# Moving the last projection of an attention stage into the next unit's first steps, and splitting the mixes by halves of the tokens

## The chip, the cores and the metric

One core of one Trainium2 chip. The metric is the device time of one execution in microseconds. The kernel before takes 2609.04 us, the median of 3 runs (2607.76 to 2612.22).

## The reference

A decoder trunk of two layers on 1024 tokens of 1024 features, in float32. Each layer computes

```python
hn = rms_norm(h, g)
proj = hn @ w_in     # q, k, v of 4 dilated heads and 4 pairs of differential heads, and cb, cc, ch
o_a = dilated_mixture_attention(aq, ak, av)           # 256 columns
o_b = rms_norm(differential_attention(...)) * scale   # 512 columns
o_c = cb * causal_dwconv(cc * ch, conv_w)             # 256 columns
h = h + concat([o_a, o_b, o_c]) @ w_out
h = h + conv_glu_ffn(rms_norm(h, g2), w_up, conv_w, w_down)
```

and a last rms_norm ends it. The change touches the attention stage, between `h @ w_in` and `@ w_out`, once per layer.

## The kernel before, in words

Everything lies with features on the 128 partitions and tokens along the free dimension; `h` is 8 tiles of 128x1024. A product in float32 is made of three passes: each operand x is rounded to a head (`x_hi`, `w_hi`) and a rest (`x_lo`, `w_lo`), and a half of a projection (`project_half`, L751: one tile of 128 output columns, one half of the tokens) is 8 x 3 = 24 matmuls of 128x512 (L747 to L749).

The mix has 8 tiles ("units"): 0 and 1 are pairs of dilated heads, 2 to 5 pairs of differential heads, 6 (`C0`) and 7 (`C1`) the gated convolution. Units 0 to 5 attend, one after the other; each takes 8 steps, one for 128 queries. `FINAL` is 5, the last attending unit. The order of work is written out by hand, one program for each engine, and the engines meet at semaphores. In a step i of unit u TensorE (`attention`, L1008) issues the scores of step i + 1 (L962, L963), turns the first group of probabilities (`turn_group`, L975), does one half of a projection for a later unit, and then attends (`attend_group`, L988). In step 0 it also turns v (L994), and in step 0 or 1 the heads of the unit before (L1004). ScalarE (L1258) copies turned probabilities out of PSUM (L1192), takes the exponentials of step i + 1 (L1233), and copies q, k, v and heads (L1200 to L1227, L1246). VectorE (L1573) masks scores and finds their top (`tops`, L1505), forms the probabilities (`shares`, L1513 to L1522), evacuates a projection's half (L1388), and between these norms the last unit's heads (`norm_heads`, L1421 to L1529), rotates q and k, makes the rests of the next unit's q and k (L1485 to L1492, after which `cur_ready` lets TensorE begin that unit's scores), and runs the convolution and its gate (`gate_out`, L1550).

`DURING` names the projections done beside unit 0 to 4, four each, two steps for each. The last is `(C1, GATED_B)`, the gate of the second convolution tile, in steps 6 and 7 of unit 4. Unit 5 has none. In its steps 2 to 7 TensorE computes the output projection of three column tiles ("early", `EARLY`) from the 7 tiles of the mix that are ready, 21 matmuls for each half (L1042). Before that the mixes must be split in head and rest in `x_hi` and `x_lo`, which the projections read until the last of them is done. GpSimd (L696 to L698, L676) splits mixes 0, 1, 2; ScalarE takes the heads (L1256) and VectorE the rests (L1554) of 3 and 6 in step 0 and 4 and 7 in step 1, all over the whole 1024 tokens, after `half_done` says that all projections are done. GpSimd otherwise splits the weight tiles in program order (`split`, L539 and L541; two slots): the first output tile before the mixes, the second right behind them. The sync queue reloads `h` behind the mix splits (`load_h`, L462) and issues the weight tiles from the third output tile on behind that.

## Time and profile before

| | us |
|---|---|
| median of 3 runs | 2609.04 |
| the profiled execution, time | 2612.52 |
| the profiled execution, span | 2610.7 |
| TensorE busy (share of the span) | 2437.4 (93%) |
| VectorE busy | 1522.6 (58%) |
| ScalarE busy | 880.9 (34%) |
| GpSimd busy | 1192.4 (46%) |
| mean granted TensorE clock | 0.967 |

Of the chain that ended last, TensorE has 69%, VectorE 20%, ScalarE 4%. Busy shares are averages over stages; what counts for a change in one stage is which wait ends last there. A wait stands in a row as "[idle before <-releaser]": the engine stood idle that long before this instruction, and what it waited for last. Names in rows are PE for TensorE, DVE for VectorE, ACT for ScalarE, POOL for GpSimd.

### The profile page before, as it was taken

The numbers are of one execution on the slowest core, as the hardware profiler recorded it, in microseconds if no ns is written. First come the engines' busy times: TensorE is split into PE (matmuls) and PEld (weight loads), VectorE is DVE, ScalarE is ACT, GpSimd is POOL, SyncE is SP. The second block draws the span as 40 slices with busy tenths as digits, with TensorE's granted clock in tenths as the row PEclk, the third lists the DMA queues.
The fourth block names the chain that finished last, engine by engine and source line by source line (L and its number), as shares of the span: only waits on it lengthen the run. The fifth ranks groups of instructions, "written<-read, shape, count | busy, mean of one in ns | idle before, by whom it ended". The sixth has DMA issues, their size and how long they took to land.

```text
span 2610.7 us, 30963 instructions
## 1 busy us (share of the span) xinstructions
PE 2437.4 (93%) x11478; PEld 2017.6 (77%) x11478; DVE 1522.6 (58%) x2161; ACT 880.9 (34%) x1667; POOL 1192.4 (46%) x786
## 2 busy tenths in 40 slices
PE   7799999797999999999989999979889999999996
PEld 6688888675788888888768888868658888888884
DVE  8544777637545555555575456774565555555546
ACT  3344444413322333332414344443232332222322
POOL 3111221347666666666421121131676666666663
PEclk9899999898999999999989999989989999999997
DMA  3000101320111111111210010112111111111111
GB/s 141 25 25 25 33 28 38 92 57 25 49 49 65 49 49 49 54 60 62 95 66 25 25 33 25 33 49 60 57 33 49 58 56 65 49 49 49 49 49 65
DMA packets 55749, 131.33 MB, mean 50 GB/s; under 512 B 4784, under 2 KB 24368, under 8 KB 55600
## 3 DMA queue, kind: packets, MB, share of 16 engines
q1 hardware_dynamic: 54016, 128.07, 15.0%
q8 instruction: 92, 1.51, 0.2%
q10 hardware_dynamic: 1584, 1.28, 0.2%
q14 instruction: 57, 0.47, 0.1%
HBM read 119.64 MB, written 9.44 MB: 49 GB/s over the span
## 4 chain that ended last, share of the span: by engine, by line
PE 69%; DVE 20%; ACT 4%; issue 3%; POOL 3%; DMA 1%; DVEq 0%; POOLq 0%; SPq 0%; ACTq 0%
PE ps L780 14%; PE ps L781 13%; PE ps L782 13%; PE ps L747 6%; PE ps L749 6%; PE ps L748 6%; PE ps L988 3%; DVE k_next L1790 3%; PE ps L975 2%; DVE h L1471 2%; PE ps L962 1%; PE ps L963 1%; ACT prob L1233 1%; DVE q_next L1446 1%; DVE h L1469 1%
## 5 line engine op out<-in xcount | busy, mean ns | idle before, releaser
L539 POOL CAST w_hi<-stage 128x1024 fp32r<-128x1024 f32 x68 | 70.7, 1040 | 859.4 <-PE ps L749 796.7
L747 PE MATMUL ps<-x_hi,w_hi 128*128 128x512 f32 x960 | 389.3, 406 | 11.3 <-POOLq L544 4.7
L574 POOL TENSOR_TENSOR w_lo<-more_stage,w_hi 128x512 fp32r<-128x512 f32 x202 | 293.7, 1454 | 209.8 <-ACT w_hi L1302 192.4
L574 POOL TENSOR_TENSOR w_lo<-stage,w_hi 128x512 fp32r<-128x512 f32 x194 | 281.4, 1451 | 214.2 <-ACT w_hi L1302 197.9
L749 PE MATMUL ps<-x_hi,w_lo 128*128 128x512 f32 x960 | 377.7, 393 | 0.0
L748 PE MATMUL ps<-x_lo,w_hi 128*128 128x512 f32 x960 | 376.7, 392 | 0.0
L1408 DVE TENSOR_TENSOR h<-ps,h 128x1024 f32<-128x1024 f32 x160 | 194.4, 1224 | 192.3 <-PE ps L782 189.0
L780 PE MATMUL ps<-T_hi,w_hi 128*128 128x512 f32 x704 | 282.0, 401 | 19.7 <-DVE T_lo L1674 6.5
L780 PE MATMUL ps<-mix,w_hi 128*128 128x512 f32 x704 | 279.3, 397 | 10.9 <-POOLq L577 5.8
L781 PE MATMUL ps<-T_lo,w_hi 128*128 128x512 f32 x704 | 279.6, 397 | 0.0
L782 PE MATMUL ps<-T_hi,w_lo 128*128 128x512 f32 x704 | 279.3, 397 | 0.0
L781 PE MATMUL ps<-mix,w_hi 128*128 128x512 f32 x704 | 276.2, 392 | 0.0
L782 PE MATMUL ps<-mix,w_lo 128*128 128x512 f32 x704 | 275.9, 392 | 0.0
L747 PEld LDWEIGHTS ps<-x_hi,w_hi 128*128 128x128 f32 x960 | 182.7, 190 | 49.8 <-issue 9.0
L780 PE MATMUL ps<-B_hi,w_hi 128*128 128x512 f32 x528 | 209.6, 397 | 4.6 <-DVE B_lo L1674 4.6
L749 PEld LDWEIGHTS ps<-x_hi,w_lo 128*128 128x128 f32 x960 | 181.8, 189 | 39.7
L748 PEld LDWEIGHTS ps<-x_lo,w_hi 128*128 128x128 f32 x960 | 182.6, 190 | 36.6 <-issue 1.2
L1302 ACT ACTIVATE w_hi<-stage 128x512 fp32r<-128x512 f32 x186 | 112.9, 627 | 287.9 <-PE ps L782 136.5
L1302 ACT ACTIVATE w_hi<-more_stage 128x512 fp32r<-128x512 f32 x188 | 113.8, 626 | 282.6 <-PE ps L782 139.9
L781 PE MATMUL ps<-B_lo,w_hi 128*128 128x512 f32 x528 | 208.2, 394 | 0.0
L782 PE MATMUL ps<-B_hi,w_lo 128*128 128x512 f32 x528 | 207.8, 394 | 0.0
L1233 ACT ACTIVATE prob<-prob,neg_top 128x128 f32<-128x128 f32 (+3 forms) x192 | 147.1, 770 | 124.6 <-DVE neg_top L1505 124.3
(200 smaller groups left out, 4582.7 us busy)
## 6 DMA issues: line engine op xcount, KB each, us to landing
stage<-stream SPq DMA_DIRECT2D x112, 512.0 KB, 3.7
more_stage<-stream SPq DMA_DIRECT2D x68, 512.0 KB, 4.3
h<-x_t SPq DMA_DIRECT2D x16, 512.0 KB, 5.5
stage<-stream SPq DMA_DIRECT2D x18, 448.0 KB, 4.6
saved_h<-h SPq DMA_DIRECT2D x8, 512.0 KB, 4.8
h<-saved_h SPq DMA_DIRECT2D x8, 512.0 KB, 3.3
out_t<-h SPq DMA_DIRECT2D x16, 256.0 KB, 2.1
stage<-stream SPq DMA_DIRECT2D x18, 64.0 KB, 4.8
```

The source lines that it names most:

```text
L574: pool.tensor_tensor(block_of(w_lo, n), raw, block_of(w_hi, n).bitcast(f32), ALU.subtract)\
L747: pe.matmul(out, w_hi[:, s, w], hi, start=start, stop=False)
L748: pe.matmul(out, w_hi[:, s, w], lo, start=False, stop=False)
L749: return pe.matmul(out, w_lo[:, s, w], hi, start=False, stop=stop)
L780: pe.matmul(out, block_of(w_hi, n)[:, columns], hi, start=start, stop=False)
L781: pe.matmul(out, block_of(w_hi, n)[:, columns], lo, start=False, stop=False)
L782: return pe.matmul(out, block_of(w_lo, n)[:, columns], hi, start=False, stop=stop)
L988: ended = pe.matmul(ps[:, HEAD, at:at + wide], turned_groups[count % 2][:, (b - b0) * P:(b - b0 + 1) * P], v_cur[:, b, dims], start=b == 0 ...
L1233: act.activation(scores, scores, ACT.Exp, bias=neg_top[:, g % 2, j:j + 1], scale=-1.0, accum_out=total[:, g % 2, j:j + 1]).then_inc(exp_do ...
L1302: act.activation(block_of(w_hi, at), raw_block(layer, n), ACT.Copy).then_inc(block_hi, 1)
L1408: dve.tensor_tensor(h[:, m, :], bank(DOWN + 2 * (m % 2), 2), h[:, m, :], ALU.add)\
L1790: dve.scalar_tensor_tensor(k_next[:, :], padded[:, PAD - back:PAD - back + SEQ], tap, k_next[:, :], ALU.mult, ALU.add).then_inc(dve_seq, 1)
```

## The change

The projection `(C1, GATED_B)` leaves steps 6 and 7 of unit 4 and becomes a unit of `DURING` of its own, done in steps 0 and 1 of unit 5, there ahead of the turning of the step's first group. VectorE evacuates it in those steps and gates each half of tile 7 by itself. The mixes are split by halves of the tokens: half 0 when the projection's first half is done, half 1 when its second is. GpSimd's part becomes two rounds of three pairs of 512 columns; the 4 heads and 4 rests of ScalarE and VectorE become 8 and 8, of which two are made in step 0 and six in step 1. The early output's half 0 waits for the half-0 splits alone, half 1 for all. The amount of work is the same; no matmul is added or left out.

```diff
--- before.py
+++ after.py
@@ -99,7 +99,8 @@
           ((2, Q), (2, K), (2, V), (C0, GATED_B)),
           ((3, Q), (3, K), (3, V), (C1, GATED_C)),
           ((4, Q), (4, K), (4, V), (C1, GATED_H)),
-          ((5, Q), (5, K), (5, V), (C1, GATED_B)))
+          ((5, Q), (5, K), (5, V)),
+          ((C1, GATED_B),))
 PROJECTIONS = BEFORE + tuple(t for unit in DURING for t in unit)
 PROJECTED = 2 * len(PROJECTIONS)
 
@@ -121,7 +122,13 @@
 LAYER_HALVES = PROJECTED + OUT_HALVES
 ATTENTION_TILES = len(PROJECTIONS) + len(OUT_TILES)
 MIX_ORDER = (0, 1, 2, 3, 6, 4, 7)
-SPLIT_BY_POOL, SPLIT_BY_ACT = (0, 1, 2), ((3, 6), (4, 7))
+
+
+SPLIT_BY_POOL = (0, 1, 2)
+SPLIT_BY_ACT = (((3, 0), (6, 0)), ((7, 0), (4, 0), (3, 1), (6, 1), (4, 1), (7, 1)))
+MIX_HALVES = SPLIT_BY_ACT[0] + SPLIT_BY_ACT[1]
+
+CONVOLVED = 3
 
 
 def projection_tile(unit, group):
@@ -460,13 +467,13 @@
                     sp.dma_start(saved_h[m * P:(m + 1) * P, :], h[:, m, :]).then_inc(h_saved[m], 16)
 
             def load_h(layer):
-                for n, m in enumerate(MIX_ORDER + (FINAL,)):
+                for m in MIX_ORDER + (FINAL,):
                     if m in SPLIT_BY_POOL:
-                        sp.wait_ge(mix_by_pool, layer * len(SPLIT_BY_POOL) + m + 1)
+                        sp.wait_ge(mix_by_pool, (2 * layer + 1) * len(SPLIT_BY_POOL) + m + 1)
                     elif m != FINAL:
-                        sp.wait_ge(mix_lo_done, layer * 4 + n - len(SPLIT_BY_POOL) + 1)
+                        sp.wait_ge(mix_lo_done, layer * len(MIX_HALVES) + MIX_HALVES.index((m, 1)) + 1)
                     else:
-                        sp.wait_ge(conv_done, (layer + 1) * C_UNITS)
+                        sp.wait_ge(conv_done, (layer + 1) * CONVOLVED)
                     rows = slice(m * P, (m + 1) * P)
                     sp.dma_start(h[:, m, :], (saved_h if layer else x_t)[rows, :]).then_inc(h_back[m], 16)
 
@@ -673,11 +680,11 @@
                         add_squares(squares[0], halves_of_t[t], 0, m)
                 pool.sem_inc(pairs_ready, 1)
 
-            def split_mix(layer, m):
+            def split_mix(layer, m, part):
                 pool.wait_ge(mix_kept, 2 * (layer * FINAL + m + 1))
-                pool.tensor_copy(x_hi[:, m, :], h[:, m, :]).then_inc(pool_seq, 1)
+                pool.tensor_copy(x_hi[:, m, part], h[:, m, part]).then_inc(pool_seq, 1)
                 pool.wait_ge(pool_seq, seen(pool_seq))
-                pool.tensor_tensor(x_lo[:, m, :], h[:, m, :], x_hi[:, m, :].bitcast(f32), ALU.subtract)\
+                pool.tensor_tensor(x_lo[:, m, part], h[:, m, part], x_hi[:, m, part].bitcast(f32), ALU.subtract)\
                     .then_inc(mix_by_pool, 1)
 
             def zeros(layer):
@@ -693,9 +700,10 @@
                     split()
                     if n == 1:
                         zeros(layer)
-                pool.wait_ge(half_done, layer * LAYER_HALVES + PROJECTED)
-                for m in SPLIT_BY_POOL:
-                    split_mix(layer, m)
+                for t in range(2):
+                    pool.wait_ge(half_done, layer * LAYER_HALVES + PROJECTED - 1 + t)
+                    for m in SPLIT_BY_POOL:
+                        split_mix(layer, m, halves_of_t[t])
                 for _ in range(len(OUT_TILES) - 3):
                     split()
                 sum_ffn(layer)
@@ -1022,19 +1030,24 @@
                             pe.wait_ge(mix_kept, 2 * (layer * FINAL + u))
                         if i < QB - 1:
                             scores(g + 1, i + 1)
+                        if u == FINAL and i < 2:
+                            if i == 0:
+                                n = next_tile()
+                            project_half(n, i, PROJ + i)
                         turn_group(g, i, dilated, layer, u, 0)
                         if i == 0:
 
                             pe.wait_ge(evac_done, first_half + PROJECTED_V[u])
                             turn_v()
-                        if u < FINAL:
+                        if u < FINAL and i < 2 * len(DURING[u]):
                             if i % 2 == 0:
                                 n = next_tile()
                             project_half(n, i % 2, PROJ + i % 2)
-                        elif i >= 2:
-                            if i == 2:
-                                pe.wait_ge(mix_by_pool, len(SPLIT_BY_POOL) * (layer + 1))
-                                pe.wait_ge(mix_lo_done, 4 * (layer + 1))
+                        elif u == FINAL and i >= 2:
+                            if i < 4:
+                                pe.wait_ge(mix_by_pool, len(SPLIT_BY_POOL) * (2 * layer + i % 2 + 1))
+                                needed = [n for n, (_, t) in enumerate(MIX_HALVES) if t == i % 2]
+                                pe.wait_ge(mix_lo_done, layer * len(MIX_HALVES) + needed[-1] + 1)
                             if i % 2 == 0:
                                 n = next_tile()
                                 ready(n)
@@ -1248,12 +1261,14 @@
                     act.activation(ps[:, HEAD, P:2 * P], ps[:, HEAD, 0:P], ACT.Square,
                                    scale=share[:, g % 2, 0:1], accum_out=head_sums[:, u // FINAL, i:i + 1]).then_inc(head_out, 1)
 
-            def split_mix(layer, m):
-                if m >= C0:
-                    act.wait_ge(conv_done, layer * C_UNITS + m - C0 + 1)
+            def split_mix(layer, m, t):
+                if m == C0:
+                    act.wait_ge(conv_done, layer * CONVOLVED + 1)
+                elif m == C1:
+                    act.wait_ge(conv_done, layer * CONVOLVED + t + 2)
                 else:
-                    act.wait_ge(mix_kept, 2 * (layer * FINAL + m + 1))
-                act.activation(x_hi[:, m, :], h[:, m, :], ACT.Copy).then_inc(mix_hi_done, 1)
+                    act.wait_ge(mix_kept, 2 * (layer * FINAL + m) + t + 1)
+                act.activation(x_hi[:, m, halves_of_t[t]], h[:, m, halves_of_t[t]], ACT.Copy).then_inc(mix_hi_done, 1)
 
             def attention(layer):
                 attended = layer * ATTENDING
@@ -1276,10 +1291,9 @@
                         if u and i == turning_step(u):
                             keep_mix(layer, u - 1)
                         if u == FINAL and i < 2:
-                            if i == 0:
-                                act.wait_ge(half_done, layer * LAYER_HALVES + PROJECTED)
-                            for m in SPLIT_BY_ACT[i]:
-                                split_mix(layer, m)
+                            act.wait_ge(half_done, layer * LAYER_HALVES + PROJECTED - 1 + i)
+                            for m, t in SPLIT_BY_ACT[i]:
+                                split_mix(layer, m, t)
                         for n in range(1, many):
                             keep_turned(g, i, dilated, n)
                             if u < FINAL and i == QB - 1 and n == max(1, many - 2):
@@ -1545,13 +1559,14 @@
                                              out[:, back:], ALU.mult, ALU.add).then_inc(dve_seq, 1)
                     dve.wait_ge(dve_seq, seen(dve_seq))
 
-            def gate_out(channel):
+            def gate_out(channel, part):
                 dve.wait_ge(evac_done, half[0])
-                dve.tensor_tensor(h[:, channel, :], gated_b, h[:, channel, :], ALU.mult).then_inc(conv_done, 1)
-
-            def split_mix(m):
+                dve.tensor_tensor(h[:, channel, part], gated_b[:, part], h[:, channel, part], ALU.mult)\
+                   .then_inc(conv_done, 1)
+
+            def split_mix(m, part):
                 dve.wait_ge(mix_hi_done, seen(mix_hi_done))
-                dve.tensor_tensor(x_lo[:, m, :], h[:, m, :], x_hi[:, m, :].bitcast(f32), ALU.subtract)\
+                dve.tensor_tensor(x_lo[:, m, part], h[:, m, part], x_hi[:, m, part].bitcast(f32), ALU.subtract)\
                    .then_inc(mix_lo_done, 1)
 
             def evacuate_projection(layer, u, i):
@@ -1605,9 +1620,9 @@
                         if u < FINAL and i == QB - 2:
                             keep_k(attended + u + 1)
                             keep_rests(attended + u + 1)
-                        if u < FINAL:
+                        if i < 2 * len(DURING[u]):
                             evacuate_projection(layer, u, i)
-                        elif i >= 2:
+                        elif u == FINAL:
                             add_out(layer, EARLY[i // 2 - 1], i % 2, PROJ + i % 2)
                         if u == 0 and i == 0:
                             rotate(q_next)
@@ -1620,16 +1635,15 @@
                         if u == 0 and i == QB - 1:
                             gate(C0)
                         if u == 1 and i == QB - 1:
-                            gate_out(C0)
+                            gate_out(C0, slice(0, SEQ))
                         if u == 3 and i == QB - 1:
                             gate(C1)
                         if u == 4 and i == 0:
                             convolve(layer, C1)
-                        if u == 4 and i == QB - 1:
-                            gate_out(C1)
                         if u == FINAL and i < 2:
-                            for m in SPLIT_BY_ACT[i]:
-                                split_mix(m)
+                            gate_out(C1, halves_of_t[i])
+                            for m, t in SPLIT_BY_ACT[i]:
+                                split_mix(m, halves_of_t[t])
                         if u < FINAL and i == QB - 1:
                             tops(layer, u + 1, 0)
                             shares(layer, u + 1, 0)
```

## Rows read from the trace of the kernel before

**Rows 1.** Timeline of PE at the end of unit 4: start us, us, engine line op, names, shapes

```profile
450.60 0.48 PE L747 MATMUL ps<-x_hi,w_hi 128*128 128x512 f32 x1
...
456.15 0.22 PE L962 MATMUL ps<-k_twice,q_split 128*128 128x128 f32 x1
...
458.77 0.38 PE L962 MATMUL ps<-k_twice,q_split 128*128 128x256 f32 x1
```

**Rows 2.** Timeline of PE in unit 5, steps 0 to 2; in brackets the wait

```profile
461.90 0.33 PE L975 MATMUL ps<-eye,prob 128*128 128x128 f32 x1 [2.40 <-DVE prob L1522]
...
464.69 0.80 PE L988 MATMUL ps<-v_cur,padded 128*128 128x128 f32 x2 [1.17 <-ACT v_cur L1200]
...
474.85 0.69 PE L975 MATMUL ps<-eye,prob 128*128 128x128 f32 x2 [8.07 <-DVE prob L1522]
...
483.61 0.76 PE L747 MATMUL ps<-x_hi,w_hi 128*128 128x512 f32 x1 [3.01 <-issue]
```

**Rows 3.** DVE and POOL in unit 5, step 0; the page's group of POOL casts

```profile
462.46 1.71 DVE L1421 TENSOR_SCALAR rs<-head_sums 128x8 f32<-128x8 f32 x1
...
465.18 0.17 DVE L1426 TENSOR_SCALAR rs<-rs 128x8 int32<-128x8 int32 x1
...
465.38 2.22 DVE L1430 SCALAR_TENSOR_TENSOR rs<-rs 128x8 f32<-128x8 f32 x1
...
465.20 2.39 POOL L680 TENSOR_TENSOR x_lo<-h,x_hi 128x1024 fp32r<-128x1024 f32 x1
...
L539 POOL CAST w_hi<-stage 128x1024 fp32r<-128x1024 f32 x68 | 70.7, 1040 | 859.4 <-PE ps L749 796.7
```

**Rows 4.** Timeline of ACT, DVE and PE, unit 5, steps 1 to 3

```profile
477.57 0.61 ACT L1233 ACTIVATE prob<-prob,neg_top 128x384 f32<-128x384 f32 x1 [1.62 <-DVE neg_top L1505]
...
479.37 0.62 DVE L1522 SCALAR_TENSOR_TENSOR prob<-prob,factor 128x384 f32<-128x384 f32 x1
...
481.15 2.36 DVE L1554 TENSOR_TENSOR x_lo<-h,x_hi 128x1024 fp32r<-128x1024 f32 x2 [1.16 <-ACT x_hi L1256]
...
486.16 0.75 DVE L1522 SCALAR_TENSOR_TENSOR prob<-prob,factor 128x512 f32<-128x512 f32 x1
...
489.79 0.83 PE L988 MATMUL ps<-v_cur,padded 128*128 128x128 f32 x6
...
492.16 0.47 PE L747 MATMUL ps<-x_hi,w_hi 128*128 128x512 f32 x1
```

**Rows 5.** Windows: stretch, us, busy of PE, PEld, DVE, ACT, POOL, PEclk, DMA share, GB/s

```profile
459.00:462.00 3.00, 0.60 (x6) 0.40 (x5) 2.27 (x4) 1.23 (x7) 2.92 (x3) 1.00 0.12 19
...
462.50:479.00 16.50, 7.25 (x29) 6.15 (x28) 14.98 (x32) 6.42 (x18) 8.33 (x5) 0.50 0.38 119
...
479.50:480.00 0.50, 0.27 (x1) 0.00 (x0) 0.49 (x1) 0.50 (x1) 0.00 (x0) 0.90 0.70 287
...
483.00:487.00 4.00, 3.39 (x9) 2.76 (x10) 2.87 (x8) 1.57 (x5) 0.00 (x0) 0.57 0.75 227
```

**Rows 6.** Timeline of ACT and DVE, unit 4, steps 6 and 7

```profile
446.89 1.06 ACT L1222 ACTIVATE q_split<-q_next 64x1024 fp32r<-64x1024 f32 x1
...
452.76 1.06 ACT L1227 ACTIVATE k_twice<-k_next 64x1024 fp32r<-64x1024 f32 x1
...
452.80 1.22 DVE L1492 TENSOR_TENSOR k_lo<-k_next,k_twice 64x1024 fp32r<-64x1024 f32 x1
```

**Rows 7.** Timeline of PE at the start of unit 4, which has projections

```profile
390.08 0.33 PE L975 MATMUL ps<-eye,prob 128*128 128x128 f32 x1 [1.54 <-DVE prob L1522]
...
405.68 0.47 PE L747 MATMUL ps<-x_hi,w_hi 128*128 128x512 f32 x1
```

**Rows 8.** DVE groups by form: line, names, shapes, xcount | busy, mean ns | idle

```profile
L1674 DVE TENSOR_TENSOR B_lo<-x_first,B_hi 128x512 fp32r<-128x512 f32 x16 | 17.6, 1152 | 0.1
...
L1674 DVE TENSOR_TENSOR T_lo<-ps,T_hi 128x512 fp32r<-128x512 f32 x24 | 16.3, 680 | 0.3
```

**Rows 9.** The page's DMA issues: names, xcount, KB each, median us to landing

```profile
stage<-stream SPq DMA_DIRECT2D x18, 448.0 KB, 4.6
```

## The prediction

> **What bounds the kernel now.** I read the chain that ended last first: it is mostly TensorE's, and in the attention units it is TensorE's order of work that sets the pace. So the question is where TensorE stands idle around the edit. All times below are of layer 0; layer 1 repeats the pattern 1280 us later, with the same waits within 0.1 us. The timeline of TensorE through the last two steps of unit 4 [rows 1] shows no gap: each half of a projection, such as the one from 450.60 to 456.15, takes 5.55 us and covers the softmax beside it. Then comes the start of unit 5, which has no projection: waits of 2.40, 1.17, 8.07 and 3.01 us [rows 2], 14.7 us in all. The 8.07 us have a cause on VectorE: the norm of unit 4's heads starts at 462.46, and its operations on 8 elements take up to 2.22 us because each stands behind a GpSimd operation of the mix splits [rows 3]. The 3.01 us are the wait for the split mixes: the last two rests end at 483.51 [rows 4]. The windows [rows 5] show the price beside the waits: TensorE's clock goes to half (0.50, which is 1.2 GHz) after 3 us with 0.60 us of work, and after the 3.01 us wait it is there again (0.57 over 483 to 487, which is half until about 486.4).
>
> **What is removed (unit 4, steps 6 and 7).** Two halves of 24 matmuls, 2 x 5.55 = 11.1 us of TensorE. They covered waits that now show. Step 6's second group needs ScalarE's copy, which stands behind the two q_split copies; these end at 447.95 [rows 6], where TensorE would be done by about 445.0: idle 3.4 us. After step 7's first transposes (449.6) TensorE must wait for the next unit's split keys: VectorE's last rest ends at 454.02, ScalarE's copy at 453.82 [rows 6]. Neither depends on the moved projection. So unit 5's first scores start at 454.2 instead of 456.15 [rows 1]: of 11.1 us only 1.95 are gained.
>
> **The clock.** Between 445.0 and 454.2 TensorE has 1.7 us of work in 9.2, sparser than the stretch that brought the clock down in [rows 5] in 3 us; I take it that it falls. It returned 2.8 us after work began (483.61 to about 486.4) and about 4.7 us after in the other case (work at 474.85, clock 0.90 in 479.5 to 480, [rows 5]). Work from 454.2 to the end of the unit is 2.62 us at full clock (456.15 to 458.77, [rows 1]), so half speed adds 1.4 to 2.35 us, and nothing if the clock holds. I take 2.2, since 4.7 us is the case that also followed long waits. TensorE then reaches unit 5's second scores at 459.0, against 458.77: unit 4 as a whole gives nothing.
>
> **What is added (unit 5, steps 0 and 1).** Unit 4's own start has just this pattern: from its first transpose at 390.08 to its third half at 405.68, 15.6 us, of which two halves are 11.1; the other work is 4.5 [rows 7]. From 459.0: scores 0.46, those 15.6, less 0.25 for the last transposes, and the wait for v, 1.17 and an end of 0.2 [rows 2]: TensorE is through the scores of step 3 at 476.2. The part behind the second half took 4.9 us at half clock (474.85 to 479.76), so 2.4 now: the second half ends at 473.8. The head norm runs meanwhile with GpSimd idle (it now waits for the first half), twelve small operations and eight scalings at 0.2 us each, 4 us instead of the 11 to 473.7, so the 8.07 us wait is gone. The 476.2 stand 3.5 us ahead of before.
>
> **The new tail.** The softmax of step 2 sits behind those transposes, and with it everything on VectorE. After 473.8: transposes and copy 0.8, exponentials to shares 1.3 (477.57 to 478.88) and 1.1 (to 479.99, [rows 4]), evacuation 0.69, half the gate 0.7, and six rests of 512 at 0.68 [rows 8], two of which half 0 needs. Without any meeting, half 0 is split at 479.8 and half 1 at 482.5. But GpSimd now splits its second halves and then a weight tile in just that time: by halving 1.04 and 2.39 us [rows 3] three pairs are an estimated 5.1 us, and the tile adds 3.4, from 474.1 on. Where such operations met before, the rests took 1152 ns on average against 680 on the same shape elsewhere [rows 8]: +0.5 us each; behind GpSimd's 1024-wide subtraction a VectorE operation lasted 2.22 [rows 3]: +2. I charge +0.5 to the mix, the gate and two rests (half 0 at 481.8), +0.5 to two more, and +0.8 and +2.0 to the two that meet the weight tile: half 1 at 487.5. TensorE starts the early output tile at 481.8 instead of 483.61, after 5 us nearly idle, so at half clock as before; with 4.9 us at full clock and 6.2 before (483.61 to 489.79, [rows 4]) I take 6.6: 488.4, and by the 2.37 us that lay between there and the next output half (489.79 to 492.16), 490.8. VectorE's own path: 487.5 + 3.4 (483.51 to 486.91, [rows 4]) + 0.4 for the transposes = 491.3. The later one counts: 491.3 against 492.16, a gain of 0.9 us. If the clock comes back sooner at 454, up to 2.2 us more pass through the same chain, 3.1. I take 1.9 per layer, 3.8 in all.
>
> Page on the meetings: the Trainium skill, "SBUF — State Buffer", section Who interferes with whom, says that a VectorE instruction with two SBUF inputs and a GpSimd instruction that reads SBUF exclude each other for the whole instruction, the first to start winning. It speaks against this change. By that rule, with strict turns, half 1 would be ready about a microsecond later than in my sum, and the time would be rival 2's below. The trace agrees in kind: the 8-element operations end with GpSimd's.
>
> **What else moves at no cost.** The sync queue loads h for the mixes behind the half-1 splits now (first about 476, last about 487.5, against 483.5) and the next weight tiles behind them; its first user is the output tile of step 6, some 15 us later, which hides it. If that cover went, the price would be one transfer, 4.6 us [rows 9]. The weight tile of the moved projection is split long before. After step 3 TensorE is the pace again, so what is gained there is kept.
>
> **Rivals.** (1) **The halves fill the gaps and the tail stays short**: VectorE and GpSimd pass each other. For it: one of the 8-element operations got in between two of GpSimd's at 0.17 us [rows 3]. Half 0 at 479.8 gives a gain of some 3.7 us per layer, and up to 7.2 if the clock holds at both places; say 4.5: 2609.0 - 9 = 2600. Against: [rows 3]. (2) **The tail eats it all**: the decisive point is the last rest of half 1. From 488.4 on (492.16 - 0.4 - 3.4) there is no gain. Full exclusion gives it: GpSimd's 8.5 us and VectorE's 5.9 (shares 0.8, gate 0.7, six rests) from 474.1, plus the 0.08 us gaps, is 488.6 to 489.1, a loss of 0.3 to 0.9 per layer; if the early tile too waits for a rest behind the 2.39 us subtraction and then runs at half clock, 3.1. Time 2609.6 to 2615.2, most likely 2611. For it: [rows 3]; against: TensorE arrives 3.5 us earlier, and the rests of [rows 8] met GpSimd at 0.5 us each, not at its whole length. (3) That nothing is moved is excluded by the order in the code.
>
> **The numbers.** The sum is against the profiled execution (span 2610.7, time 2612.5), so 2608.7 there; the runs' median is 2609.04, 3.5 lower, and I apply the difference to it: 2605.2. A measurement here can tell about 0.2% (5.2 us) from no change. Forecast (gain 0.5 to 3.3 per layer) 0.50, rival 1 0.18, rival 2 0.32. Beyond 0.2% faster means over 2.6 per layer: rival 1 and 0.22 of the forecast, 0.40. Slower by 0.2% is rival 2's far end, 0.14. The rest, 0.46, is within. The range takes in rival 1's likely time and most of rival 2: 2599.5 to 2613.5.
>
> **What would show it.** Right: TensorE idle 3 to 5 us twice between 445 and 454 with the clock at 0.50 by 454; first moved half at about 459.5, no wait of 8 us at step 1, VectorE's 8-element operations at 0.17 us; then a wait of about 5 us before the first output half, and VectorE's rests of 512 at 1.0 to 2.7 us. Wrong: a clock of 1.00 through 454, or rests at 0.68 us (rival 1); the third output step starting later than 492.2 (rival 2).

## The result, and the profile after

The changed kernel takes 2616.74 us (median of 13 runs, 2611.62 to 2618.67) against 2611.03 us before (13 runs, 2607.76 to 2614.13): the ratio is 1.0018, with a 95% interval of 1.0011 to 1.0025. It is slower, by 2.9 to 6.5 us, where 2605.2 was forecast and 2613.5 was the upper end of the range. The profiled execution of the changed kernel took 2613.8 us (span 2611.8). That is 2.9 us below its median, and the one of before (2612.52 us) lies 1.5 above its own, so I compare the two traces stretch by stretch and not by their whole length.

The page's busy times hardly differ from before:

```profile
PE 2436.4 (93%) x11478; PEld 2016.8 (77%) x11478; DVE 1514.2 (58%) x2171; ACT 881.7 (34%) x1675; POOL 1195.7 (46%) x798
```

The chain that ended last shows where to look. GpSimd has 5% of it, against 3% before:

```profile
PE 68%; DVE 19%; POOL 5%; ACT 4%; issue 3%; DMA 1%; DVEq 0%; POOLq 0%; SPq 0%; ACTq 0%
```

Followed in order of time through steps 1 and 2 of unit 5 in layer 0 (start us, us, what), it runs over GpSimd's splits of the second half of the tokens. Of the 4.83 us behind them it shows only "issue", which is time with no releaser in the profile, so other timelines have to tell what they are:

```profile
472.46 0.62 POOL x_hi L685
473.15 1.28 POOL x_lo L687
...
477.29 1.27 POOL x_lo L687
478.57 4.83 issue
483.39 0.77 PE ps L755
```

Each kernel reaches unit 4 at a slightly different time, so I set all of them to one mark M ahead of everything that the change touches, a wait of about 1 us for ScalarE's copy that every kernel has. Here are the mark and the waits of TensorE in the timeline of the changed kernel; they answer to [rows 1] and [rows 2]:

```profile
429.44 0.49 PE L996 MATMUL ps<-v_cur,padded 128*128 128x128 f32 x2 [0.99 <-ACT padded L1205]
...
446.79 0.45 PE L996 MATMUL ps<-v_cur,padded 128*128 128x128 f32 x1 [3.29 <-ACT padded L1205]
...
452.40 0.48 PE L970 MATMUL ps<-k_twice,q_split 128*128 128x128 f32 x1 [3.24 <-DVEq L1509]
...
457.90 0.39 PE L755 MATMUL ps<-x_hi,w_hi 128*128 128x512 f32 x1
...
465.69 0.49 PE L996 MATMUL ps<-v_cur,padded 128*128 128x128 f32 x2 [1.18 <-ACT v_cur L1213]
...
476.80 0.55 PE L983 MATMUL ps<-eye,prob 128*128 128x128 f32 x3 [1.95 <-DVE prob L1536]
...
483.39 0.77 PE L755 MATMUL ps<-x_hi,w_hi 128*128 128x512 f32 x1 [6.05 <-issue]
...
490.38 0.83 PE L996 MATMUL ps<-v_cur,padded 128*128 128x128 f32 x6
...
492.75 0.47 PE L755 MATMUL ps<-x_hi,w_hi 128*128 128x512 f32 x1
```

And the mark in the kernel before:

```profile
431.14 0.49 PE L988 MATMUL ps<-v_cur,padded 128*128 128x128 f32 x2 [0.99 <-ACT padded L1192]
```

The first output half starts at M + 53.95 (483.39 - 429.44), before at M + 52.47 (483.61 - 431.14, [rows 2]); the output half of step 3, behind which TensorE is the pace again, at M + 63.31 against M + 61.02 ([rows 4]: 492.16). So 2.3 us are lost in layer 0. By the same marks layer 1 loses 2.6 (M + 63.65 against M + 61.05). That makes 4.9 in both, against 5.7 between the medians.

The clock behaved as forecast. I call a wait bare where no projection covers it. In these windows (columns as in [rows 5]) it is at 0.50, which is 1.2 GHz, after the two bare waits of unit 4, and again after the 6.05 us wait:

```profile
440.00:450.00 10.00, 5.10 (x29) 4.09 (x27) 7.95 (x12) 6.83 (x13) 1.11 (x1) 0.85 0.00 0
450.00:456.00 6.00, 3.60 (x17) 3.60 (x18) 2.90 (x7) 3.41 (x7) 0.00 (x0) 0.50 0.01 3
...
457.50:465.00 7.50, 7.01 (x38) 5.76 (x36) 4.36 (x24) 1.45 (x5) 1.32 (x2) 1.00 0.00 0
...
479.00:482.00 3.00, 0.00 (x0) 0.00 (x0) 3.00 (x3) 1.62 (x5) 2.92 (x2) 0.50 0.66 221
...
484.00:488.00 4.00, 4.00 (x11) 3.13 (x10) 3.02 (x8) 1.52 (x4) 0.00 (x0) 0.51 0.75 258
```

What TensorE waits for lies on VectorE. Its timeline in the norm and in the tail, which answers to [rows 3] and [rows 4]:

```profile
459.28 0.17 DVE L1444 SCALAR_TENSOR_TENSOR rs<-rs 128x8 f32<-128x8 f32 x1
...
461.08 1.66 DVE L1543 TENSOR_SCALAR heads<-heads,rs 128x128 f32<-128x128 f32 x8
...
475.03 1.71 DVE L1536 SCALAR_TENSOR_TENSOR prob<-prob,factor 128x384 f32<-128x384 f32 x1
476.67 0.68 DVE L1402 TENSOR_TENSOR h<-ps,rstd_all 128x512 f32<-128x512 f32 x1
477.38 1.73 DVE L1564 TENSOR_TENSOR h<-h 128x512 f32<-128x512 f32 x1
479.03 6.67 DVE L1569 TENSOR_TENSOR x_lo<-h,x_hi 128x512 fp32r<-128x512 f32 x6
```

The last row merges the six rests. In narrower windows they come apart, into the first, the second and the four of the second half of the tokens:

```profile
479.03 1.52 DVE L1569 TENSOR_TENSOR x_lo<-h,x_hi 128x512 fp32r<-128x512 f32 x1
...
480.47 2.82 DVE L1569 TENSOR_TENSOR x_lo<-h,x_hi 128x512 fp32r<-128x512 f32 x1
...
483.21 2.48 DVE L1569 TENSOR_TENSOR x_lo<-h,x_hi 128x512 fp32r<-128x512 f32 x4
```

and GpSimd's in the same stretch:

```profile
475.06 1.27 POOL L687 TENSOR_TENSOR x_lo<-h,x_hi 128x512 fp32r<-128x512 f32 x1
476.27 0.94 POOL L685 CAST x_hi<-h 128x512 fp32r<-128x512 f32 x1
477.29 1.26 POOL L687 TENSOR_TENSOR x_lo<-h,x_hi 128x512 fp32r<-128x512 f32 x1
478.50 1.50 POOL L546 CAST w_hi<-stage 128x1024 fp32r<-128x1024 f32 x1
480.08 2.66 POOL L548 TENSOR_TENSOR w_lo<-stage,w_hi 128x1024 fp32r<-128x1024 f32 x1
```

The norm is clean: the operation that took 2.22 us beside GpSimd [rows 3] takes 0.17. The price is at the end. The probabilities of step 2 take 1.71 us (0.62 in [rows 4]), the gate's half 1.73, and of the six rests the first two take 1.52 and 2.82, the other four 0.68 each. The first two are what the first output half needs. GpSimd's subtraction of the weight tile ends at 482.74, the second rest at 483.29, and TensorE starts at 483.39: the second rest stood behind the subtraction.

### The profile page after: what moved, and what is told of

It is laid out like the page before. It is cut to its first block, busy times and chain, and to the rows that moved or that the text cites. A ratio compares the mean times of both kernels' runs of the same rounds, so it can differ in the third digit from the quotient of the medians.

```text
span 2611.8 us, 30999 instructions
## 1 busy us (share of the span) xinstructions
PE 2436.4 (93%) x11478; PEld 2016.8 (77%) x11478; DVE 1514.2 (58%) x2171; ACT 881.7 (34%) x1675; POOL 1195.7 (46%) x798
## 3 DMA queue, kind: packets, MB, share of 16 engines
q1 hardware_dynamic: 54016, 128.07, 14.8%
q8 instruction: 92, 1.51, 0.2%
## 4 chain that ended last, share of the span: by engine, by line
PE 68%; DVE 19%; POOL 5%; ACT 4%; issue 3%; DMA 1%; DVEq 0%; POOLq 0%; SPq 0%; ACTq 0%
PE ps L788 13%; PE ps L789 13%; PE ps L790 13%; PE ps L755 6%; PE ps L757 6%; PE ps L756 6%; PE ps L996 4%; DVE k_next L1804 3%; PE ps L983 2%; DVE h L1485 2%; PE ps L970 2%; PE ps L971 1%; ACT prob L1246 1%; DVE q_next L1460 1%; POOL w_lo L581 1%
```

## The experiments

Three theories were put against each other first. **A**: the tail loses because GpSimd's operations, the weight tile's above all, stand between VectorE's. **B**: the loss is TensorE's, the bare waits of unit 4 and the half clock behind them. **C**: it lies elsewhere. All times are medians, of 5 to 13 runs; each ratio is to 9 to 30 runs of the kernel before on the same chip (M + ... is read in layer 0). The kernel before itself differs by up to 3.2 us between these chips, so two rows from different chips are compared by their ratios.

| kernel | us | ratio, 95% interval | first output half | output half of step 3 |
|---|---|---|---|---|
| before | 2609.6 to 2612.8 | 1 | M + 52.47 | M + 61.02 |
| changed | 2616.7 | 1.0018 (1.0011 to 1.0025) | M + 53.95 | M + 63.31 |
| x1_tile_late | 2609.6 | 1.0000 (0.9991 to 1.0009) | M + 51.06 | M + 60.28 |
| x2_pool_yields | 2603.2 | 0.9976 (0.9966 to 0.9986) | M + 48.62 | M + 57.89 |
| x3_warm | 2610.2 | 1.0001 (0.9993 to 1.0010) | M + 51.76 | M + 60.70 |
| x4_both | 2603.6 | 0.9970 (0.9958 to 0.9981) | M + 46.31 | M + 55.58 |
| x5_one_half | 2602.0 | 0.9965 (0.9953 to 0.9978) | M + 48.30 | M + 57.58 |
| x6_warm_tail | 2610.1 | 0.9991 (0.9982 to 0.9999) | M + 54.01 | M + 61.24 |
| a1_whole_wait | 2625.5 | 1.0054 (1.0042 to 1.0067) | M + 56.37 | M + 66.22 |
| m1_move_alone | 2631.0 | 1.0073 (1.0058 to 1.0088) | M + 61.60 | M + 70.41 |
| b1_norm_first | 2608.1 | 0.9998 (0.9989 to 1.0007) | M + 52.23 | M + 60.86 |
| b2_halves | 2603.7 | 0.9970 (0.9960 to 0.9979) | M + 49.41 | M + 56.68 |
| b3_late_halves | 2599.9 | 0.9957 (0.9941 to 0.9973) | M + 46.00 | M + 55.69 |
| b4_tile_late | 2596.0 | 0.9945 (0.9931 to 0.9958) | M + 46.64 | M + 53.89 |

Twice the difference in the last column gives the difference of the medians within 2 us or so, in all but three: a1_whole_wait and x6_warm_tail, whose medians lie 4.6 us above and 3 below it, and x4_both, whose median shows 4 us less gain than it.

**x1_tile_late** (the changed kernel; GpSimd keeps the next weight tile back until all mixes are split):

```diff
                         split_mix(layer, m, halves_of_t[t])
+                pool.wait_ge(mix_lo_done, (layer + 1) * len(MIX_HALVES))
                 for _ in range(len(OUT_TILES) - 3):
```

> The kernel after, but GpSimd waits for the last of VectorE's rests before it splits the next weight tile. Theory A (the loss is GpSimd's 1024-wide weight split falling between VectorE's rests on half 0): the second rest ends about 2.3 us sooner, the first early output half starts 2.3 us sooner or more, the last rest ends 3 us sooner; about 3 us per layer back, 2610 to 2611 where the kernel after has 2616.7. Theory B (the loss is the two bare waits in unit 4 and the half clock behind them): no change, 2616 to 2617. Theory C (the loss lies elsewhere, in later stages): no change either, and the output half starts sooner without effect on the time.

The loss comes back in full: the ratio falls from 1.0018 to 1.0000, which is about 5 us, and step 3's output half comes 3.0 us sooner in layer 0 and 3.3 in layer 1. The six rests take 3.69 us, not 6.67, and TensorE starts the first output half 2.9 us sooner:

```profile
480.58 3.69 DVE L1570 TENSOR_TENSOR x_lo<-h,x_hi 128x512 fp32r<-128x512 f32 x6
```

**x2_pool_yields** (x1_tile_late; GpSimd's second halves wait until VectorE has split the first four of its own):

```diff
+                    if t:
+                        pool.wait_ge(mix_lo_done, layer * len(MIX_HALVES) + 4)
                     for m in SPLIT_BY_POOL:
```

> As the kernel before this one, and GpSimd also begins its half-1 mix splits only after the half-0 rests are done, so that no GpSimd work lies beside the softmax of step 2, the gate and the first two rests. Theory A: the first early output half starts 3.5 to 4 us sooner than in the kernel after (at about 479.5 on its trace); the four rests of half 1 take about 4 us more than bare but the output half hides them; 3 to 4 us per layer back, about 2609 to 2610. Theory B: 2616 to 2617.

Another 6.4 us on the same chip, and the moved projection is now in a kernel that beats the one before. That is more than I had expected (2609 to 2610): the first output half starts 5.3 us sooner than in the changed kernel. The wait for the probabilities falls from 1.95 to 0.54 us, the gate's half from 1.72 to 0.69, and the wait for the splits from 3.06 to 2.03:

```profile
476.88 0.55 PE L986 MATMUL ps<-eye,prob 128*128 128x128 f32 x3 [0.54 <-DVE prob L1539]
479.46 0.77 PE L758 MATMUL ps<-x_hi,w_hi 128*128 128x512 f32 x1 [2.03 <-issue]
```

Theory A holds. It doesn't exclude B.

**x3_warm** (the changed kernel; 15 matmuls of 128x512, whose result nobody reads, in each of steps 6 and 7 of unit 4):

```diff
+                        elif u == FINAL - 1:
+                            s = ready(tile[0])
+                            take_bank(PROJ + i % 2)
+                            for k in range(15):
+                                pe.matmul(bank(PROJ + i % 2), w_hi[:, s, 0:P], x_hi[:, k % KT, 0:HALF],
+                                          start=True, stop=True)
```

> The kernel after with 15 matmuls of 128x512, whose result nobody uses, in each of the two steps of unit 4 that lost their projection (the work is added, nothing is left out). They fit in the waits. Theory B: TensorE's clock stays at full speed into unit 5 (granted 1.00 from 450 to 457), the second scores of unit 5 start about 2 us sooner, and the time falls by 2 us per layer, to about 2612 to 2613. Theory A: the 2 us pass through the same chain of softmax, gate and rests, so the same fall shows, but the 6 us wait at the first output half stays as long as it is, and the start of that half moves by the same 2 us only.

The useful scores of unit 5 start no sooner (M + 22.98, M + 22.96 without the fillers), and what follows runs at full clock: the product with v, 465.69 in the changed kernel, comes 2.19 us earlier against the mark:

```profile
464.61 0.49 PE L996 MATMUL ps<-v_cur,padded 128*128 128x128 f32 x2 [1.17 <-ACT v_cur L1219]
```

At step 3 it is 2.6 us in layer 0 and 2.9 in layer 1, and 4.4 us in all by the ratios. So B holds as well: two losses each as large as the whole. That is no contradiction. The change has a gain too (the 8.07 us wait), and these losses more than use it up.

**x4_both** (x2_pool_yields with x3_warm's matmuls):

> The changed kernel with GpSimd's weight tile and second mix halves held back as in x2_pool_yields (2603.2), and with the 15 unused matmuls of x3_warm in steps 6 and 7 of unit 4. If the meetings on VectorE and the half clock after unit 4's bare waits are two separate losses, both come back: x3_warm gave 3.3 us per layer where VectorE was late; in x2_pool_yields the wait before the first output half is 2.03 us, so an arrival 2 to 3 us sooner is paid back only in part. 2598 to 2601 if they add in part, 2603 (no change from x2_pool_yields, the wait of 2.03 us growing to 4 to 5) if VectorE is then the pace of the tail.

At the step-3 half the gains add (M + 55.58 against 57.89), but the median is x2_pool_yields' own. The two ran on different chips, their intervals overlap, and the traced execution of x4_both (2599.3 us) lies 4.3 below its median. So I can't say whether the 2.3 us per layer arrive at the end.

**x5_one_half** (x2_pool_yields, but the first half of the projection stays in step 6 of unit 4 and only the second is moved, to step 0 of unit 5; TensorE's part):

```diff
-                        if u == FINAL and i < 2:
-                            if i == 0:
-                                n = next_tile()
-                            project_half(n, i, PROJ + i)
+                        if u == FINAL and i == 0:
+                            project_half(n, 1, PROJ + 1)
...
+                        elif u == FINAL - 1 and i == 6:
+                            n = next_tile()
+                            project_half(n, 0, PROJ)
```

> As x2_pool_yields, but only the second half of the projection is moved, to step 0 of unit 5; the first half stays in step 6 of unit 4. Of unit 4's bare waits of 3.29 and 3.24 us the first should be covered and the second stay; in unit 5 no projection stands in step 1, so a wait for the probabilities of 2 to 4 us comes back there, but the mixes' splits may begin a step sooner. If the wait is only moved between the units: 2603 as x2_pool_yields. If the earlier splits pay: 2599 to 2601. If the step without cover costs more than it saves: 2606 to 2609.

The wait is moved rather than removed. Step 6 is covered, but ahead of unit 5's scores TensorE waits 5.78 us instead of 3.52, and a wait of 0.75 us comes in step 1. By the trace the 5.78 us have the same cause as the losses in the tail: GpSimd's first splits now begin at 445.89, beside VectorE's four rests of the next unit's q and k. These take 1.51, 2.17, 1.51 and 2.18 us, where each takes 1.22 in the changed kernel, and the scores wait for the last of them. By the ratios, 0.9965 and 0.9976 with overlapping intervals, there is no clear gain on x2_pool_yields.

```profile
451.63 2.18 DVE L1510 TENSOR_TENSOR k_lo<-k_next,k_twice 64x1024 fp32r<-64x1024 f32 x1
...
453.92 0.48 PE L973 MATMUL ps<-k_twice,q_split 128*128 128x128 f32 x1 [5.78 <-DVEq L1513]
```

**x6_warm_tail** (the changed kernel; 20 such matmuls just ahead of the 6.05 us wait; they read the weight tile alone):

```diff
+                            if i == 2:
+                                n = next_tile()
+                                s = ready(n)
+                                take_bank(PROJ)
+                                for k in range(20):
+                                    pe.matmul(bank(PROJ), w_hi[:, s, 0:P], w_hi[:, s, 0:HALF], start=True, stop=True)
...
```

> The changed kernel with 20 unused matmuls of 128x512 (0.22 us each at full clock, 4.3 us) just before the wait of 6.05 us that ends with the first output half. If TensorE's half clock there (7.0 us for that output half, against 4.9 at full clock) is part of the loss: the half lasts about 5 us and 3 to 4 us come back, 2612 to 2614. If the end of VectorE's rests sets what follows (its path from the last rest through the probabilities of step 3): 2615 to 2617, no change. If the fillers run at half clock themselves they last 8.6 us and it is 5 us slower.

The first output half starts no sooner (M + 54.01), but lasts 5.0 us (485.21 to 490.24), not 7.0 (483.39 to 490.38), and step 3's is 2.1 us earlier. After the fillers, which themselves ran partly at half clock (0.64 over 480 to 484), the clock is at 1.00 where it was at 0.51:

```profile
480.00:484.00 4.00, 4.00 (x13) 3.10 (x13) 4.00 (x3) 1.61 (x5) 3.92 (x3) 0.64 0.64 226
484.00:488.00 4.00, 4.00 (x18) 3.08 (x17) 4.00 (x6) 0.00 (x0) 0.56 (x1) 1.00 0.29 84
```

This shows that TensorE's own path, and not VectorE's rests, sets step 3 in the changed kernel. The changed kernel's trace agrees: VectorE's probabilities of step 3 end at 489.10, 1.3 us before TensorE is through its output half (490.38).

**a1_whole_wait** (the changed kernel; the first output half waits for all splits):

```diff
-                                pe.wait_ge(mix_by_pool, len(SPLIT_BY_POOL) * (2 * layer + i % 2 + 1))
-                                needed = [n for n, (_, t) in enumerate(MIX_HALVES) if t == i % 2]
+                                pe.wait_ge(mix_by_pool, len(SPLIT_BY_POOL) * (2 * layer + 2))
+                                needed = [len(MIX_HALVES) - 1]
```

> The changed kernel, but the first output half also waits for all the mix splits, not for its own half of the tokens. By my reading half 0 is ready at 483.4 and half 1 at about 485.7 of the changed kernel's clock: TensorE starts 2.4 us later per layer. If that start decides the next steps, 4 to 5 us slower than the changed kernel (2616.7), at 2621; if the end of VectorE's last rest decides them, less than 1.5 us slower; if the halves cost more than they give (more and shorter instructions), no slower at all.

TensorE starts 2.4 us later, as expected, and the wait is 8.46 us. The loss at step 3 is 2.9 us per layer. By the ratios the kernel is 9.4 us slower, and their intervals leave 6 to 13: twice 2.9 lies at the edge. The two traced executions are 7.2 us apart. Whether something else costs time here stays open.

**m1_move_alone** (the kernel before; the projection moved, the mixes whole):

```diff
-SPLIT_BY_POOL, SPLIT_BY_ACT = (0, 1, 2), ((3, 6), (4, 7))
+SPLIT_BY_POOL, SPLIT_BY_ACT = (0, 1, 2), ((), (3, 6, 4, 7))
...
+                        if u == FINAL and i < 2:
+                            if i == 0:
+                                n = next_tile()
+                            project_half(n, i, PROJ + i)
...
-                            if i == 0:
+                            if i == 1:
                                 act.wait_ge(half_done, layer * LAYER_HALVES + PROJECTED)
...
-                        if u == 4 and i == QB - 1:
+                        if u == FINAL and i == 1:
                             gate_out(C1)
```

> The kernel before with the projection moved into steps 0 and 1 of the last unit and nothing else: the mixes are split whole (1024 tokens) once both halves are projected, and all output halves wait for all of them. The two parts of the change are then known singly. Splitting by halves alone took 6.8 us off (b2_halves, 2603.7 against 2610.5); if the parts add up, moving alone costs 12 to 13 us: 2622 to 2624. If the halves are worth more in the moved kernel, where nothing else covers the splits (all of GpSimd's three pairs, 10.2 us, now start at the end of the second half): 2626 to 2632. If the move is in itself near neutral and the loss came from the way the halves collide: 2610 to 2615.

**b2_halves** (the other part alone: the changed kernel with the projection back in unit 4, everything else by halves; the gate of tile 7 too stays in steps 0 and 1 of unit 5, where the change put it):

```diff
-          ((5, Q), (5, K), (5, V)),
-          ((C1, GATED_B),))
+          ((5, Q), (5, K), (5, V), (C1, GATED_B)))
...
-                    pool.wait_ge(half_done, layer * LAYER_HALVES + PROJECTED - 1 + t)
+                    pool.wait_ge(half_done, layer * LAYER_HALVES + PROJECTED)
```

> The kernel before with the mixes split by halves of the tokens and the first output half waiting for its own half alone; the projection stays at the end of unit 4. Theory A: GpSimd's operations of 0.6 and 1.3 us instead of 1.04 and 2.39 let VectorE's norm through sooner, so the wait of 8.07 us falls to 5 to 7, and the wait before the first output half goes from 3.01 to 1 to 2: 2601 to 2607. The rival: twelve instructions more on the three engines, with the same time of GpSimd in all, move the waits about and leave 2608 to 2611.

These two runs take the change apart. The move alone makes the kernel 18.3 us slower; the halves alone, with the gate's new place, make it 6.8 faster. What the gate's place is worth by itself was not run: the first wait of unit 5 is 1.52 us in b2_halves and 2.40 in [rows 2]. The halves are worth more once the projection is moved, since the difference of the ratios, 1.0073 and 1.0018, is 14 us. In the kernel with the move alone TensorE waits 13 us in the tail, because four rests of 1024 (an estimated 1.2 us each by [rows 4], where two take 2.36) take 10.59 us in turns with GpSimd's last mix pair and the weight tile's:

```profile
479.37 10.59 DVE L1559 TENSOR_TENSOR x_lo<-h,x_hi 128x1024 fp32r<-128x1024 f32 x4
```

```profile
490.06 0.77 PE L748 MATMUL ps<-x_hi,w_hi 128*128 128x512 f32 x1 [12.99 <-issue]
```

In b2_halves the 8 us wait of [rows 2] is still there, with 8.44 us, but the tail is short:

```profile
473.76 0.69 PE L982 MATMUL ps<-eye,prob 128*128 128x128 f32 x2 [8.44 <-DVE prob L1531]
...
480.42 0.47 PE L754 MATMUL ps<-x_hi,w_hi 128*128 128x512 f32 x1 [1.03 <-issue]
```

The first line of VectorE here is the scaling of the heads. The first of the eight begins at 469.00 beside GpSimd's subtraction of the weight tile (468.82 to 471.16) and takes 2.25 us, the other seven 0.28 each. The second line is the six rests, with GpSimd idle:

```profile
469.00 3.62 DVE L1538 TENSOR_SCALAR heads<-heads,rs 128x128 f32<-128x128 f32 x8
...
479.03 3.70 DVE L1564 TENSOR_TENSOR x_lo<-h,x_hi 128x512 fp32r<-128x512 f32 x6
```

**b1_norm_first** (the kernel before; GpSimd's splits wait for the norm):

```diff
                 pool.wait_ge(half_done, layer * LAYER_HALVES + PROJECTED)
+                pool.wait_ge(heads_ready, layer * B_UNITS + FINAL - A_UNITS)
                 for m in SPLIT_BY_POOL:
```

> The kernel before, in which GpSimd waits with the mix splits until the head norm of unit 4 is done on VectorE. If the 8.07 us wait of step 1 is GpSimd standing in the way of VectorE's small operations, the norm takes about 4 us, the wait falls to 1 us or less, and TensorE turns the heads some 7 us sooner; the mix splits then meet VectorE's rests of 1024, and the first output half starts 1 to 4 us sooner: 2603 to 2609 against 2611. If the wait has another cause, it stays at about 8 us and the time rises by the delay of the mix splits, 2 to 5 us per layer.

The 8.07 us wait becomes 4.15, not 1 or less as expected, and three waits of 2.48, 3.04 and 3.56 us stand behind it, for the tops, the probabilities and the splits: nothing is gained. This is the change's own pattern without its move: what is taken from the norm meets the softmax and the rests.

```profile
466.11 0.69 PE L976 MATMUL ps<-eye,prob 128*128 128x128 f32 x2 [4.15 <-DVE prob L1523]
...
471.85 0.50 PE L963 MATMUL ps<-k_twice,q_split 128*128 128x512 f32 x1 [2.48 <-DVE neg_top L1506]
...
476.10 0.90 PE L976 MATMUL ps<-eye,prob 128*128 128x128 f32 x3 [3.04 <-DVE prob L1523]
...
480.56 0.77 PE L748 MATMUL ps<-x_hi,w_hi 128*128 128x512 f32 x1 [3.56 <-issue]
```

**b3_late_halves** (b2_halves; GpSimd's second halves wait for the norm, the weight tile for all splits) and **b4_tile_late** (b2_halves with the weight tile's wait alone, the line of x1_tile_late):

```diff
                     pool.wait_ge(half_done, layer * LAYER_HALVES + PROJECTED)
+                    if t:
+                        pool.wait_ge(heads_ready, layer * B_UNITS + FINAL - A_UNITS)
```

> b2_halves (2603.7), and GpSimd's splits of the second half of the tokens wait until the head norm is through, the weight tile's until all mixes are split. Theory A: the norm, which has three more GpSimd operations beside it in b2_halves, meets half as many; the wait of 8.44 us falls to 4 to 6, and what GpSimd then does beside the probabilities and rests gives 1 to 2 back: 2599 to 2602. The rival: the meetings only move from the norm to the rests, as in b1_norm_first, where a wait of 8.07 became 4.15 and two others took its place: 2603 to 2606.

> b2_halves (2603.7) with GpSimd's splits of the weight tile held back until all mixes are split, and nothing else: the one of the two parts of b3_late_halves (2599.9) that x1_tile_late had in the changed kernel. In b2_halves the tile's two operations (467.71 to 471.16) lie beside the eight scalings of the heads, which take 3.62 us against 1.66 in the changed kernel, where GpSimd is idle. If meetings alone explain it: the wait of 8.44 us falls by 1.5 to 2 and 2600 to 2601 comes out, so that holding back the second halves adds little in b3_late_halves. If the tile's place does not matter here: 2603 to 2605, and b3_late_halves owes its gain to the halves.

b4_tile_late has the lowest median and ratio of all: 2596.0 us, 14.8 less than before on the same chip, and a larger gain than I had expected (2600 to 2601). The scalings take 1.66 us again and the wait is 6.57 us (5.69 in layer 1):

```profile
465.85 1.66 DVE L1539 TENSOR_SCALAR heads<-heads,rs 128x128 f32<-128x128 f32 x8
```

```profile
468.64 0.69 PE L983 MATMUL ps<-eye,prob 128*128 128x128 f32 x2 [6.57 <-DVE prob L1532]
...
475.30 0.47 PE L755 MATMUL ps<-x_hi,w_hi 128*128 128x512 f32 x1 [1.36 <-issue]
```

Holding the second halves back as well shortens the wait further, to 4.01 us, but brings others (0.94 and 1.24), and step 3 comes 1.8 us later than in b4_tile_late: by the marks the one line is enough. By the medians the two are not told apart, since their intervals overlap.

## Why the prediction was wrong

**Right: what the removal leaves.** Bare waits of 3.4 us and up to the scores at 454.2 were forecast; they are 3.29 and 3.24 us, and the scores start at M + 22.96, which is 454.1 in the times of the prediction (M is 431.14 there). The half clock was put at 2.2 us, and x3_warm gives 2.19 at the product with v.

**Right: the path to the end of the moved projection.** Its second half was to end at 473.8 and ended at M + 42.8, or 473.9. The norm's operations fell to 0.17 us each, and the wait of 8.07 us is gone.

**Near as a total, by luck in part: VectorE's rests.** The last of half 1 was put at 487.5 and ended at 487.4 (485.70 in the changed kernel's times). But the forecast's own terms add up to 488.3 (482.5 + 2.0 + 1.0 + 2.8), so 0.8 us was left out of the sum. With it VectorE's path would have been at 492.1 and the gain 0.1 us, not 0.9. Measured against bare operations, the meetings cost 5.4 us, where the terms have 5.8 and the sum used 5.0.

**Wrong: the step that charged "+0.8 and +2.0 to the two that meet the weight tile" to half 1.** The sizes were right and the place was wrong. The two rests that met the tile took 1.52 and 2.82 us, 0.84 and 2.14 over the bare 0.68, and they were the two of half 0; the four of half 1 met nothing. The forecast's own times say so already: they put half 0's rests at 479.4 to 481.8, and GpSimd's weight tile at 479.2 to 482.6. The 0.5 us charged to each meeting was also too little ahead of them. The probabilities of step 2 lost 1.1 us (1.71 against 0.62), the small operation before them 0.3 (0.54 against 0.22) and the gate's half 1.0 (1.73 against 0.69 in x2_pool_yields), where 1.0 was charged in all. So half 0 was ready at 485.0 and TensorE started at 485.1, not 481.8. The errors in the total nearly cancelled; which half they hit decides when TensorE starts. x1_tile_late shows the size: without the weight tile there the start is M + 51.06, which is 482.2 against the forecast 481.8, and step 3 comes at M + 60.28, 491.4 against 491.3.

**Wrong in consequence: "VectorE's own path: 491.3" as the later of the two.** A start at 485.1 and 7.0 us at half clock (6.6 were forecast) put TensorE's path at the end, at 494.5. x6_warm_tail shows it: with the clock up, and with VectorE's rests where they were, 2.1 us come back.

**A choice without ground:** the sum as it stood gave a gain of 0.9 us per layer and I took 1.9. Where the forecast's own path was met, in x1_tile_late, step 3 gains 0.74 us per layer, and the median doesn't differ from that of before.

**Rival 2 happened**, near its far end, in the form that the prediction named: "the early tile too waits for a rest behind the 2.39 us subtraction and then runs at half clock". It priced this at 3.1 us per layer; 2.3 and 2.6 were measured at step 3, and 2.9 between the medians. Its main form, a last rest at 488.4 or later, did not happen (487.4). It was held back for a reason that the trace did not carry: the average of 1152 ns in [rows 8] is that of another stretch with another order of operations, and averages say nothing about which single operation waits. In that very stretch (589.9 to 604.6 us in the trace of before) the single rests take from 0.68 to 1.78 us. The Trainium skill ("SBUF — State Buffer", section Who interferes with whom) states the exclusion for the whole of an instruction; the trace agrees, since operations of VectorE of 0.62 and 0.68 us took 1.71 and 1.73 where one of GpSimd's of 1.27 and 1.26 us began within 0.1 us of them. Which of two wins can't be read off the starts when they are this close: the probabilities begin at 475.03, 0.03 us before GpSimd's subtraction at 475.06, and yet end 0.4 us after it.

**Not seen at all:** that the two parts of the change pull in opposite directions. I costed them together. Alone, the halves (with the gate's new place) are 6.8 us faster and the move 18.3 slower. The move takes the cover from unit 4, and puts the splits, on which the output tiles wait, behind the work that used to run beside them.

**Open:** whether a1_whole_wait costs more than the 5.8 us that step 3 accounts for; whether x4_both's earlier step 3 reaches the end; what the gate's place is worth; and whether b3_late_halves and b4_tile_late differ. A single trace settles none of these: ahead of the mark, where no edit reaches, the traced executions differ by 3.9 us among themselves (M lies between 427.3 and 431.2).

## What to carry to other kernels

When VectorE and GpSimd both work out of SBUF, the on-chip memory that holds these tiles, in a tail, lay out their operations one by one in the order in which they will alternate, and look at which one stands ahead of the first consumer; a total, or an average from another stretch, can be right and still miss the start. Ask next which of GpSimd's operations in that stretch is not urgent: one wait that kept the next weight tile back gave, by the ratios, about 5 and 6.5 us in the two kernels it was added to alone. And cost each part of a change by itself: here one part was worth having and the other was not.

## What the runs showed that was not expected

- The scalings of the heads (TENSOR_SCALAR on 128x128, one large input) are slowed by GpSimd too: 3.62 us for eight where the first stands behind the weight tile's subtraction, 1.66 with GpSimd idle. The evacuation out of PSUM was not: 0.68 us at 476.67 beside GpSimd's cast, and 0.69 at 451.68 in b4_tile_late, where GpSimd is idle. GpSimd's cast at 476.27 itself took 0.94 us against 0.61; VectorE's probabilities were under way when it began.
- TensorE's half clock is a price of its own that a longer wait brings along: about 2.2 us behind unit 4's waits and about 2 behind the 6.05 us wait, both bought back with matmuls that compute nothing.
- Two single remedies (x1_tile_late, x3_warm) each gave back about what the change had cost, and a third (x6_warm_tail) did too. A remedy that restores the time does not show that it removed the only cause.
